# The order of work around six layer norms in a one-core hybrid encoder step

## What is computed

```python
x = _layer_norm(ALPHA * x + 0.5 * _swiglu(x, ffn1_gate, ffn1_up, ffn1_down), ln1_g, ln1_b)
proj = x @ w_mix_in            # conv branch, and queries/keys/values of a sparse attention
mix = concat([y_conv, y_attn]) @ w_mix_out
x = _layer_norm(ALPHA * x + mix, ln2_g, ln2_b)
x = _layer_norm(ALPHA * x + _mem_attention(x, mem_k, mem_v, w_mem_q, w_mem_o), ln3_g, ln3_b)
x = _layer_norm(ALPHA * x + 0.5 * _swiglu(x, ffn2_gate, ffn2_up, ffn2_down), ln4_g, ln4_b)

def _layer_norm(x, g, b):
    mu = x.mean(-1); var = square(x - mu).mean(-1)
    return (x - mu) * rsqrt(var + LN_EPS) * g + b
```

## Time and profile before

| | |
|---|---|
| median of 3 runs | 2529.94 us (2528.02 to 2529.94) |
| profiled execution | 2529.03 us |
| its span, first to last instruction | 2527.1 us |
| PE busy | 2437.4 us, 96% |
| PEld (weight loads) busy | 88% |
| POOL busy | 54% |
| ACT busy | 39% |
| DVE busy | 36% |
| mean granted TensorE clock | 0.993 |

### The profile page before, as it was taken

One profiled execution on the slowest core, in us unless ns is written; L12 is line 12 of the kernel. 1 busy time (PEld: TensorE's weight loads), 2 busy tenths in 40 slices (PEclk: granted clock), 3 DMA queues, 4 the chain that ended last, 5 costly groups with the idle time before them and its releaser, 6 DMA issues.

```text
span 2527.1 us, 39958 instructions
## 1 busy us (share of the span) xinstructions
PE 2437.4 (96%) x16311; PEld 2216.2 (88%) x16311; DVE 920.0 (36%) x1775; ACT 982.0 (39%) x1736; POOL 1376.1 (54%) x860
## 2 busy tenths in 40 slices
PE   8999999999999999998999999999889999999998
PEld 8888889888999999987789877888659899999998
DVE  1000002266800004277442699996364333000003
ACT  4333333543333233445543533323463435333231
POOL 4777665534666665422252676766404346666663
PEclk9999999999999999999999999999999999999999
DMA  4444532453233232533121233333402122433322
GB/s 146 123 118 117 160 92 79 136 155 103 84 93 92 84 87 78 143 103 131 38 76 34 77 99 101 118 91 94 166 1 85 50 68 82 120 109 101 92 84 69
DMA packets 425661, 245.00 MB, mean 97 GB/s; under 512 B 23008, under 2 KB 415328, under 8 KB 424720
## 3 DMA queue, kind: packets, MB, share of 16 engines
q1 hardware_dynamic: 389712, 197.88, 27.5%
q10 hardware_dynamic: 33200, 32.56, 4.0%
q0 software_dynamic: 2576, 12.07, 1.3%
HBM read 218.79 MB, written 21.74 MB: 95 GB/s over the span
## 4 chain that ended last, share of the span: by engine, by line
PE 83%; ACT 5%; DVE 4%; POOL 3%; DMA 2%; issue 2%; ACTq 0%; DVEq 0%; POOLq 0%
PE LIN L762 76%; POOL WL L2077 2%; PE TR L1091 1%; PE LIN L839 1%; ACT WH L1143 1%; PE TR L815 1%; POOL XL L2117 1%; ACT PR L1592 1%; ACT PT L1617 1%; PE LIN L1039 1%; PE TR L916 1%; DVE SC L1698 1%; DVE PR L2016 1%; DVE CB L1942 1%; PE TR L1078 1%
## 5 line engine op out<-in xcount | busy, mean ns | idle before, releaser
L2077 POOL TENSOR_TENSOR WL<-WRAW,WH 128x1024 fp32r<-128x1024 f32 (+1 forms) x378 | 889.5, 2356 | 474.4 <-ACT WH L1143 468.3
L762 PE MATMUL LIN<-XH,WH 128*128 128x256 f32 (+3 forms) x3032 | 837.6, 317 | 20.8 <-DVE Y L1766 6.4
L762 PE MATMUL LIN<-XH,WL 128*128 128x256 f32 (+3 forms) x3032 | 830.2, 314 | 0.0
L762 PE MATMUL LIN<-XL,WH 128*128 128x256 f32 (+3 forms) x3032 | 828.9, 314 | 0.0
L762 PEld LDWEIGHTS LIN<-XH,WH 128*128 128x128 f32 (+1 forms) x3032 | 528.3, 188 | 61.2 <-issue 20.4
L762 PEld LDWEIGHTS LIN<-XL,WH 128*128 128x128 f32 (+1 forms) x3032 | 528.2, 188 | 34.0
L762 PEld LDWEIGHTS LIN<-XH,WL 128*128 128x128 f32 (+1 forms) x3032 | 526.1, 188 | 33.8
L762 PE MATMUL LIN<-HH,WH 128*128 128x256 f32 (+2 forms) x1632 | 464.3, 307 | 1.7 <-POOL HL L2158 1.7
L762 PE MATMUL LIN<-HL,WH 128*128 128x256 f32 (+2 forms) x1632 | 462.1, 305 | 0.0
L762 PE MATMUL LIN<-HH,WL 128*128 128x256 f32 (+2 forms) x1632 | 461.4, 305 | 0.0
L1147 ACT ACTIVATE FG<-LIN 128x512 f32<-128x512 f32 (+3 forms) x270 | 154.9, 575 | 738.3 <-PE LIN L762 730.4
(11 more groups left out here) (200 smaller groups left out, 2049.4 us busy)
## 6 DMA issues: line engine op xcount, KB each, us to landing
WRAW<-in_ffn_gate SPq DMA_DIRECT2D x88, 512.0 KB, 3.7
WRAW<-in_ffn_up SPq DMA_DIRECT2D x88, 512.0 KB, 3.7
WRAW<-in_ffn_down SPq DMA_DIRECT2D x64, 512.0 KB, 3.8
WRAW<-in_w_mix_in SPq DMA_DIRECT2D x44, 512.0 KB, 3.8
WRAW<-in_ffn_down SPq DMA_DIRECT2D x32, 384.0 KB, 3.3
WRAW<-in_w_mix_out SPq DMA_DIRECT2D x16, 512.0 KB, 3.9
WRAW<-in_w_mem_q SPq DMA_DIRECT2D x16, 512.0 KB, 3.9
WRAW<-in_w_mem_o SPq DMA_DIRECT2D x16, 512.0 KB, 3.9
```

The costliest lines, as they stand in the source:

```text
L762: last = pe.matmul(LIN[0:pr.rows, pr.slot, out:out + w], wt[:, pr.tile % RING, c, 0:pr.rows], x[:, c, col:col + w], start=(c == 0 and wt i ...
L2077: pool.tensor_tensor(WL[:, n % RING, 0:nk, 0:width], WRAW[:, n % 2, 0:nk, 0:width], WH[:, n % RING, 0:nk, 0:width].bitcast(F32), ALU.subtr ...
```

## The change

1. At half 0 of each of the six norms, the steps for chunks 4 and 5 (7 and 8) are hung behind the last product j7 of half 1 instead of in its middle, so VectorE and ScalarE consume j7 first. The last addition of squares is taken after those two steps and ahead of steps 9 and 10.
2. ScalarE takes the weight split of j6 and of j7 (tiles n and n+1) behind its `end` strands: behind step 6, and behind steps 7 to 10 (and 11, where there is one).
3. GpSimd no longer splits at j6 and j7. It splits tiles n and n+1 after the next pair, whose middle holds half 1's step 0: behind the root, and behind what it does to consume the pair. Elsewhere GpSimd now splits ahead of the `end` strands.

```diff
+def late_split(pr):
+    return any(strand[0] == "norm" and strand[2] == 0 and strand[3] >= 6 for strand in pr.end)
...
-        at(3, "mid", 7, 8)
-        at(3, "end", 9, 10)
+        if h == 0:
+            at(3, "end", 7, 8)
+            four[3].end.append(("last square", four[3].p))
+            at(3, "end", 9, 10)
+        else:
+            at(3, "mid", 7, 8)
+            at(3, "end", 9, 10)
...
 # ScalarE
-                            if pr.last and not (pr is products[-1] and PLAN.segments[s + 1:] and
+                            if pr.last and not late_split(pr) and not (pr is products[-1] and PLAN.segments[s + 1:] and
                                                 PLAN.segments[s + 1][0] == "load"):
                                 split_hi(pr.tile + RING, pr)
                         for pr in prs:
                             for strand in pr.end:
                                 take_up(strand)
+                            if late_split(pr):
+                                split_hi(pr.tile + RING, pr)
...
 # VectorE
-                if pr.j == KD - 1:
+                if pr.j == KD - 1 and h == 0:
                     add_square(pr, pr.j)
...
+                elif kind == "last square":
+                    add_square(PLAN.products[what[0]], KD - 1)
...
 # GpSimd
-                        normed_first = any(strand[0] == "norm" for pr in prs for strand in pr.end)
-                        for ends in (True, False) if normed_first else (False, True):
-                            for pr in prs:
-                                if not ends and pr.last:
-                                    split_lo(pr.tile + RING)
-                                for strand in pr.end if ends else ():
-                                    take_up(strand)
+                        if any(strand[0] == "norm" and strand[2:] == (1, 0) for pr in prs for strand in pr.mid):
+                            split_lo(prs[0].tile + 2)
+                            split_lo(prs[0].tile + 3)
+                        for pr in prs:
+                            if pr.last and not late_split(pr):
+                                split_lo(pr.tile + RING)
+                        for pr in prs:
+                            for strand in pr.end:
+                                take_up(strand)
```

## The result

The changed kernel takes **2552.49 us** (median of 4 runs, 2549.23 to 2555.81) against 2529.49 us for the kernel before (4 runs beside it, 2528.02 to 2529.94): ratio 1.0089, 95% interval 1.0077 to 1.0101. It is slower by 0.9%, 23 us, where 15 were forecast; the time is 2.5 us above the upper end of the range. The profiled execution took 2555.81 us, its span is 2553.9, and the mean granted clock 0.985.

What follows compares the result with a forecast made beforehand. TensorE, busy 96% of the span, was taken as the bound. Terms 4.0 + 5.9 + 5 = 14.9 us on the profiled 2529.03 gave 2543.9, so 2544.8 us for the median; range 2531 to 2550.

Steps and rivals of the forecast that it cites:

- the clock's: TensorE's clock behind the longer norm stops: five drops at 1.2 us less one, +5 us.
- The stops at norms 0, 1, 2 and 4: Two `DIAG` each wait out a whole GpSimd split: +0.9 or +1.1 us per norm, +4.0 us for four.
- the further 0.3 us: Norm 0: `MSQ` and `VAR` less drawn out by GpSimd's `XL`, gaining 0.3 us, variance at 452.95.
- Norms 3 and 5: Feed-forward norms: TensorE waits for tile n, split only after GpSimd consumes the pair: +3.1 and +2.75, together +5.9 us.
- pass 6 stood behind that split and isn't ready that early, 0.4 us of idle time: ScalarE at norm 3: reordered work leaves 0.4 us idle before pass 6, so `FG` ends at 1430.3.
- The stops in sum: Longer TensorE stops at all six norms, without the clock: +9.9 us.
- The read of j7 first: At each norm TensorE's pair starts 0.78 us earlier (0.5 with 288 columns); waits for Y fall from 9.8 to some 6.
- The case where the clock holds: Stops get longer and nothing else changes: 2540 us, chance 0.14.
- `DIAG` waiting once: At norms 0, 1, 2, 4 the second `DIAG` precedes split n+1: 2532 us; chance 0.14 shared with no hold-up.
- Faster: Late splits don't hold TensorE at any norm, most norm stops go: 2514 us, chance 0.08.
- What the loads do: SP's load of tile n+3 goes out some 8 us later, with 12 us to land in: hidden.

Runs made afterwards that it cites:

- `filled`: Changed kernel with idle matmuls, whose results are never read, inside TensorE's stops at the six norms: 2539.33 us.
- `split_before_use`: Changed kernel with GpSimd splitting tiles n and n+1 right behind the root, ahead of its consumption of the pair, altering norms 3 and 5 only: 2543.57 us.
- `root_between`: Changed kernel with GpSimd splitting tile n at j6 behind its strands, then root, split n+1, consumption, with no wait for `DIAG`: 2528.05 us.
- `wait_diag`: Changed kernel with GpSimd waiting after the root for all `DIAG` before it splits tiles n and n+1: 2536.09 us.
- `root_between_wait`: Changed kernel with GpSimd splitting tile n at j6, then root, wait for all `DIAG`, split n+1, consumption: 2517.53 us.
- `act_early`: Changed kernel with ScalarE's two weight splits back in their old place ahead of its passes: 2546.52 us.
- `before_filled`: Kernel before the change with 14 idle matmuls in each of its six stops for `DIAG`: 2530.20 us.

## Why the prediction was wrong in size and right in kind

**The step that failed is the clock's**: "From below it costs nothing more, from above six times 1.5 us less the one there is; I take five drops at 1.2 less one: +5 us". Even its upper bound, some 8 us, was too low. PE's busy time rose by 15.6 us in the profiled execution, and `filled` gave back 13.2 between medians. All six stops dropped the clock, not five, and each drop cost more: held against `filled`, the busy time at norms 0 to 5 was 1.4, 2.9, 2.2, 2.3, 2.8 and 2.4 us more, 2.3 on average where I had taken 1.2 from norm 2 of the kernel before. The loss has two parts. The spreading matmuls at the end of the stop are slow, 0.80 us at norm 0 for the last two where I had counted 0.35, and so are the first of the 48 matmuls behind it. The length of the stop alone does not set the price: norms 1 and 4 with stops of 3.5 and 3.3 us lost more than norms 3 and 5 with 7.4 and 6.9. What does set it stays open. The Trainium skill, page "TensorE: Matmul & The Clock Gate", section "Why this matters for your kernels", warns that longer gaps between bursts drop the clock to its half, and all six did here; the other kernels show no clean line by length. At norm 2 of `split_before_use` stops of 3.3 us together left the clock at 1.00, and at norm 4 of `root_between` one of 1.6 us did not (0.72 in the 6 us behind it). With six drops at my price the term would have been 6: the price, not the count, was the larger error.

**The stops at norms 0, 1, 2 and 4** were forecast at +0.9 and +1.1 each; by idle time they were +0.9 and +0.6. The mechanism held: at norm 0 both `DIAG` took 4.66 us (4.8 forecast), the first ended with split n and the second with split n+1. `wait_diag`, `root_between` and `root_between_wait` show it as cause: with GpSimd held back by 0.6 us the two take 0.48. The Trainium skill, page "SBUF — State Buffer", section "Who interferes with whom", says that the one who comes second waits for the whole instruction of the other; the trace agrees for each `DIAG` by itself, and adds that the second `DIAG` is again the second comer. Output 2 started 1.8 us later than before (459.84 against 458.08) rather than 0.9: 0.2 of it had been there ahead of the norm, and some 0.45 is the slow spreading matmuls, which belong to the clock. The root came at 453.58, not at 452.95. `MSQ` took 0.73 and `VAR` 0.58 (0.76 and 0.47 before), still beside GpSimd's `XL`, which ran from 450.33 to 453.47, so the further 0.3 us that I had counted as gain were not there. It did little harm, since the two `DIAG` then took 0.3 us less than forecast.

**Norms 3 and 5** were forecast at +5.9 us with a new wait of about 6 us each for WL. The waits were 7.4 and 6.9, and idle time grew by 4.0 and 3.7 us, 7.7 together: the forecast was short by about 1 us each. The step is "pass 6 stood behind that split and isn't ready that early, 0.4 us of idle time": ScalarE stood idle for 0.3 and 0.6 us before its passes at 1430.57 and 1433.34, and `FG` came late by it. `act_early` puts the splits back and the two waits fall by 2.1 us together, to 12.2. That the chain `FP`, `HH`, `HL`, split has no slack, and that `DIAG` costs nothing there, was right.

**The stops in sum**: 9.9 forecast, 10.7 by idle time at the norms, 11.9 by the waits. This part of the prediction held, though in part by luck: norms 1 and 4 came out 1.0 us below the forecast together and norms 3 and 5 1.8 above.

**The read of j7 first**: the waits for Y went from 9.8 to 5.6, 6 forecast. Alone it changed no time measurably.

**The rivals.** The case where the clock holds (2540) is what `filled` makes real, at 2539.33. So the two parts of the sum, the longer stops and a clock term apart from them, were the right two. `DIAG` waiting once (2532) is refuted by the 4.66 us. Faster (2514) hung on whether split n would end before 455.2 at norm 0; the two splits ran from 454.27 to 458.91, so n ended after 456. Nearest to it came `root_between_wait`, where that split runs before the root: 2517.53.

**What the loads do**, forecast hidden, does not show in PE's waits.

**Left open**: what sets the price of a drop, and why the clock drops in some executions in attention and the first feed-forward and not in others (2525.68 to 2533.02 over 11 runs of `before_filled`). Of the profiled 15.6 us of busy time 13.8 lie at the norms, in agreement with the 13.2 between the medians, and 2.6 between norms 1 and 2; elsewhere it fell by 0.8. That the 2.6 are such a drop by chance and not a consequence of the change is argued, not tested.

## What to carry to other kernels

When an instruction is moved ahead on one engine, look at what its queue does next, because that now runs beside the consumer of the result. A short wait put in front of it can be worth far more than it costs (0.6 us of GpSimd at each of six norms against 10.5 us of the kernel). When a stop of TensorE grows, price the clock apart from the stop, as a range and not from a single drop, and measure it by filling the stop with idle matmuls. The busy time of the same number of matmuls, before and after, tells both at a glance. And where a late piece of work is only put elsewhere in its queue, ask who is queued behind its new place.

## What was not expected of the hardware

- A drop of the clock cost 1.4 to 2.9 us of busy time at the six norms of the changed kernel (held against `filled`), and the longest stops were not the dearest: 2.9 us behind a stop of 3.5 us at norm 1, 2.3 behind one of 7.4 at norm 3. In `root_between` a stop of 1.6 us at norm 4 was enough for a drop.
- Two `DIAG` of 0.28 us each, back to back on VectorE, lost their turn twice to GpSimd's next split of 2.4 us. At these norms the engines took turns: one split got in ahead of each of the first two `DIAG`, and with three `DIAG` (4.87 us at norm 1) the third went through once GpSimd had no further split.
- VectorE's `CSUM` took 1.01 us beside GpSimd's `XL` of 0.74, against 0.43 where it began first (before, at 447.85; there `XL` began 0.08 us later and took 0.95).
